# A hybrid decoder layer on one core: gate strips ahead of branch strips, the recurrence's last step behind the convolution, and evenly spaced head steps

## The reference

```
xn = rmsnorm(x)
p  = xn @ w_in                      # 2048 x 13328, split into xl, gl, q, k, v, z, b, a, u_pool, three gates
xl = causal_conv(xl, width 4)       # then the RG-LRU recurrence h_t = a_t h_{t-1} + b_t
o_lru  = h * gelu(gl)
o_dn   = gated delta rule over 8 heads of 128, on conv'd q, k, v, then a norm and silu(z)
o_pool = causal means over 2, 4, 8, 16 tokens, a grouped product, a scale
merged = sum over the three branches of sigmoid(gate_b) * (o_b @ w_back_b)
x = x + merged @ w_out
x = x + square(relu(rmsnorm(x) @ w_up)) @ w_down
y = rmsnorm(x)                      # and the states of all branches
```

## Time and profile before

| what | us |
|---|---|
| median of 3 runs | 2188.42 (2185.13 to 2188.83) |
| the profiled execution | 2186.87 |
| its span in the trace | 2185.1 |
| PE busy (products) | 2149.7, 98% of the span |
| DVE / ACT / POOL busy | 1222.3 / 784.2 / 175.9 |
| granted clock of PE, mean over the span | 0.994 |
| first gated pass (RG-LRU branch) | from about 324 |
| second gated pass (pooling branch) | from about 654 |

### The profile page before, as it was taken

The page is one execution under the profiler, slowest core; times in us unless marked ns, Lnnn a source line. Parts: engine busy times, 40 slices in busy tenths (PEclk is TensorE's granted clock), DMA queues, the critical chain, the costliest instruction groups (busy, mean ns, idle before and its releaser), DMA issues.

```text
span 2185.1 us, 35787 instructions
## 1 busy us (share of the span) xinstructions
PE 2149.7 (98%) x14515; PEld 2094.4 (96%) x14515; DVE 1222.3 (56%) x1996; ACT 784.2 (36%) x946; POOL 175.9 (8%) x340
## 2 busy tenths in 40 slices
PE   9999998999999999999999999999999999999997
PEld 9998997999998999999999999999999999999997
DVE  7996785555566655555454554444444444444444
ACT  6434553222232222333334343333333333333343
POOL 7000012110022110010000000000000000000001
PEclk9999999999999999999999999999999999999998
DMA  6544443343353433336544444444444444444443
GB/s 218 163 143 128 140 129 121 116 119 116 116 165 106 118 117 116 116 107 212 150 148 155 145 144 152 147 153 146 154 145 154 146 154 146 154 145 154 147 144 106
DMA packets 295609, 308.96 MB, mean 141 GB/s; under 512 B 9712, under 2 KB 290416, under 8 KB 295232
## 3 DMA queue, kind: packets, MB, share of 16 engines
q1 hardware_dynamic: 291616, 291.54, 43.1%
q0 software_dynamic: 3584, 15.55, 2.4%
q10 hardware_dynamic: 288, 0.15, 0.0%
HBM read 298.83 MB, written 8.37 MB: 141 GB/s over the span
## 4 chain that ended last, share of the span: by engine, by line
PE 84%; DVE 9%; ACT 3%; issue 3%; DMA 1%; DVEq 0%; ACTq 0%; SPq 0%
PE main L1436 26%; PE main L1438 25%; PE main L1437 25%; PE aux L1556 6%; DVE scratch L892 2%; DVE lo L885 2%; DVE scratch L885 2%; ACT hi L617 1%; DMA raw<-in_w_in 1%; DVE scratch L889 1%; PE aux L1539 0%; PE aux L1529 0%; DVE scratch L888 0%; DVE merged L885 0%; PE aux L1660 0%
## 5 line engine op out<-in xcount | busy, mean ns | idle before, releaser
L885 DVE TENSOR_TENSOR lo<-raw,hi 128x1024 fp32r<-128x1024 f32 x546 | 667.2, 1230 | 566.6 <-ACT hi L617 560.0
L617 ACT ACTIVATE hi<-raw 128x1024 fp32r<-128x1024 f32 x546 | 573.3, 1056 | 920.6 <-PE main L1438 904.8
L1436 PE MATMUL main<-x_hi,hi 128*128 128x320 f32 x2688 | 842.8, 314 | 2.5 <-DVE x_lo L892 2.0
L1438 PE MATMUL main<-x_hi,lo 128*128 128x320 f32 x2688 | 831.5, 309 | 0.0
L1437 PE MATMUL main<-x_lo,hi 128*128 128x320 f32 x2688 | 831.5, 309 | 0.0
L1436 PEld LDWEIGHTS main<-x_hi,hi 128*128 128x128 f32 x2688 | 505.7, 188 | 10.6 <-issue 5.0
L1437 PEld LDWEIGHTS main<-x_lo,hi 128*128 128x128 f32 x2688 | 505.8, 188 | 0.7
L1438 PEld LDWEIGHTS main<-x_hi,lo 128*128 128x128 f32 x2688 | 505.4, 188 | 0.0
L1436 PE MATMUL main<-o_hi,hi 128*128 128x320 f32 x1408 | 444.6, 316 | 4.6 <-DVE o_lo L885 4.6
L1438 PE MATMUL main<-o_hi,lo 128*128 128x320 f32 x1408 | 435.6, 309 | 0.0
L1437 PE MATMUL main<-o_lo,hi 128*128 128x320 f32 x1408 | 435.5, 309 | 0.0
(11 more groups left out here) (253 smaller groups left out, 1190.8 us busy)
## 6 DMA issues: line engine op xcount, KB each, us to landing
raw<-in_w_in SPq DMA_DIRECT2D x210, 512.0 KB, 3.8
raw<-in_w_up SPq DMA_DIRECT2D x128, 512.0 KB, 3.8
raw<-in_w_down SPq DMA_DIRECT2D x128, 512.0 KB, 3.4
raw<-in_w_back SPq DMA_DIRECT2D x80, 512.0 KB, 3.4
scratch<-in_s_in POOLq DMA_DIRECT2D x8, 512.0 KB, 4.7
out_s_out<-scratch POOLq DMA_DIRECT2D x8, 512.0 KB, 4.6
merged<-in_x SPq DMA_DIRECT2D x8, 320.0 KB, 7.8
qkv<-in_x POOLq DMA_DIRECT2D x1, 2560.0 KB, 10.2
```

Source lines behind the costliest of these rows:

```text
L617: act.activation(HI[:, slot * TILE:(slot + 1) * TILE], RAW[:, slot * TILE:(slot + 1) * TILE], ACT.Copy).then_inc(hi_ready, 1)
L885: return dve.tensor_tensor(out, a, b, op)
L1436: pe.matmul(bank, hi, xh, start=first, stop=False)
L1438: return pe.matmul(bank, lo, xh, start=False, stop=last)
```

## The change

It does four things.

1. In a gated turn both gate strips run first (tiles 0 to 3 and 4 to 7, banks 0, 1 and 2, 3), then both branch strips (tiles 8, 9 and 10, 11). There is a gate buffer for each strip; the rows RN and BG now lie in the first. Gate 0 and gate 1 are at keys 8 and 12, merge 0 and merge 1 at keys 2 and 4 of the next turn. SP's loads follow that order.
2. In the recurrence part step 5 moves from key 7 to key 8, on DVE behind `lru_conv`, on ACT behind the split that stands at key 7 already (`walk_ahead` has none left at key 8). Turn 3's steps, which run in the first gated turn, keep key 7.
3. The 19 steps of head i of a pass are placed by a formula in tiles of the whole pass, 5.5 + 10.9 i for k0, + 0.8 for k1, + 2.1 for k2, then 0.48 a step from + 2.6. Heads no longer coincide with turns.
4. The loops over turns 1 to 3 of the first two gated passes are written out on PE, ACT and DVE.

```diff
-        GS = sb("gate", 2 * N)
-        RN, BG = sb("qk_scale_rows", N), sb("beta_gamma_rows", N)
+        GS, GS1 = sb("gate", 2 * N), sb("gate_second", 2 * N)
+        GATE = (GS, GS1)
+        RN, BG = GS[:, 0:N], GS[:, N:2 * N]
...
             def gated(it, n0, name):
                 for s in range(2):
                     for j in range(4):
-                        load(n0, 12, it, 6 * s + j, A["w_in"], j * 512, it * 512 + (G0[name] + s * 256))
+                        load(n0, 12, it, 4 * s + j, A["w_in"], j * 512, it * 512 + (G0[name] + s * 256))
+                for s in range(2):
                     for j in range(2):
-                        load(n0, 12, it, 6 * s + 4 + j, A["w_back"], BACK[name] + j * 512, it * 512 + s * 256)
+                        load(n0, 12, it, 8 + 2 * s + j, A["w_back"], BACK[name] + j * 512, it * 512 + s * 256)
...
-        def lru_steps(step, it):
+        def lru_steps(step, it, last=7):
 
             return {pos: [lambda k=k: step(it, k) for k in ks]
-                    for pos, ks in ((3, (0,)), (4, (1,)), (5, (2, 3)), (6, (4,)), (7, (5,)))}
+                    for pos, ks in ((3, (0,)), (4, (1,)), (5, (2, 3)), (6, (4,)), (last, (5,)))}
...
-        def dn_place(k, peeled):
-
-
-            if peeled and k < 14:
-                return ((5, 3), (6, 1), (6, 4), (6, 6), (7, 0), (7, 2), (7, 4), (7, 6), (7, 7),
-                        (8, 1), (8, 2), (8, 4), (8, 6), (8, 7))[k]
-            if k < 6:
-                return ((1, 7), (2, 5), (3, 7), (4, 2), (4, 5), (4, 7))[k]
-            return (5 + (k - 6) // 2, (3, 7)[k % 2]) if k < 18 else (11, 6)
-
-        def dn_steps(step, h, peeled, late):
+        def dn_place(i, k):
+
+            at = 5.5 + 10.9 * i + ((0.0, 0.8, 2.1)[k] if k < 3 else 2.6 + 0.48 * (k - 3))
+            eighth = int(round(8 * at))
+            return (eighth - 1) // 8, (eighth - 1) % 8
+
+        def dn_steps(step, h0, it):
 
             steps = {}
-            for k in range(19):
-                pos = dn_place(k, peeled)[0] + 4
-                if (pos > 12) == late:
-                    steps.setdefault(pos - 12 * late, []).append(lambda k=k: step(h, k))
+            for i in range(4):
+                for k in range(19):
+                    at = dn_place(i, k)[0] + 4 - 12 * it
+                    if 0 < at <= 12:
+                        steps.setdefault(at, []).append(lambda i=i, k=k: step(h0 + i, k))
             return steps
...
-                lru(it, lru_steps(lru_step, it - 1))
+                lru(it, lru_steps(lru_step, it - 1, 8))
...
-                walk(split, LRU_N, 8, it, 8, {**after, 8: [lambda: lru_conv(it)]})
+                walk(split, LRU_N, 8, it, 8, joined({8: [lambda: lru_conv(it)]}, after))
...
-            def gated(it, n0, t0, g0, h0, branch, after, peeled=False):
-                own = {8: [lambda: gate(n0, t0, it, 0)], 10: [lambda: merge(n0, t0, g0, it, 0, branch)]}
+            def gated(it, n0, t0, g0, h0, branch, after):
+                own = {8: [lambda: gate(n0, t0, it, 0)], 12: [lambda: gate(n0, t0, it, 1)]}
                 if h0 is not None:
-                    own = joined(own, dn_steps(dn_step, it + h0, peeled, False))
+                    own = joined(own, dn_steps(dn_step, h0, it))
                 walk(split, n0, 12, it, 12, joined(after, own))
 
             def late(it, n0, t0, g0, h0, branch):
 
-                steps = {2: [lambda: gate(n0, t0, it, 1)], 4: [lambda: merge(n0, t0, g0, it, 1, branch)]}
-                return steps if h0 is None else joined(steps, dn_steps(dn_step, it + h0, False, True))
+                steps = {2: [lambda: merge(n0, t0, g0, it, 0, branch)], 4: [lambda: merge(n0, t0, g0, it, 1, branch)]}
+                return joined(steps, dn_steps(dn_step, h0, 4)) if h0 is not None and it == 3 else steps
...
                 for s in range(2):
-                    strip(n0, 12, t0, 8, it, 6 * s, 4 * s, XH, XL, between=between)
-
-                    strip(n0, 12, t0, 8, it, 6 * s + 4, 4 * s + 2, OH, OL,
+                    strip(n0, 12, t0, 8, it, 4 * s, 2 * s, XH, XL, between=between)
+                for s in range(2):
+                    strip(n0, 12, t0, 8, it, 2 * s + 8, 2 * s + 4, OH, OL,
                           waits=(lambda i: (o_ready, o0 + 2 * (i + 1))) if first is not None and s == 0 else None,
                           tiles=2, between=between)
 
-            gated(0, GPL_N, GPL_T, 0, 4, 0)
-            with pe.Fori(1, 4) as it:
+            gated(0, GPL_N, GPL_T, 0, 4, 0, dn_first=4)
+            for it in range(1, 4):
                 gated(it, GPL_N, GPL_T, 0, None, 0)
```

More of the change, by code:

```diff
@@ L767, in dn_step, with gated @@
                     act.activation(S1, AX[2][:, 0:P], ACT.Copy).then_inc(s1_ready, 1)
-            def gated(it, n0, t0, h0, after, peeled=False):
-                own = {8: [lambda: gate(it, 0, t0, 0)]}
-                if h0 is not None:
-                    own = joined(own, dn_steps(dn_step, it + h0, peeled, False))
-                walk(split, n0, 12, it, 12, joined(after, own))
-            def late(it, t0, h0):
-                steps = {2: [lambda: gate(it, 1, t0, 0)]}
-                return steps if h0 is None else joined(steps, dn_steps(dn_step, it + h0, False, True))
-            gated(0, GPL_N, GPL_T, 0, lru_steps(lru_step, 3), True)
-            with act.Fori(1, 4) as it:
-                gated(it, GPL_N, GPL_T, 0, late(it - 1, GPL_T, 0))
+            def gated(it, n0, t0, h0, after):
+                own = {8: [lambda: gate(it, 0, t0, 0)], 12: [lambda: gate(it, 1, t0, 0)]}
+                walk(split, n0, 12, it, 12, joined(after, joined(own, dn_steps(dn_step, h0, it))))
+            gated(0, GPL_N, GPL_T, 0, lru_steps(lru_step, 3))
+            for it in range(1, 4):
+                gated(it, GPL_N, GPL_T, 0, {})
             def pool_hi(g):
@@ L786, in pool_hi @@
                 act.activation(OH[:, 2 * g * N:2 * (g + 1) * N], DD, ACT.Copy).then_inc(ohi_ready, 1)
[L788 to L791, removed]
+            walk(split, POOL_N, 16, 0, 16, {**dn_steps(dn_step, 0, 4), 12: [lambda: pool_hi(0)], 16: [lambda: pool_hi(1)]})
+            gated(0, GPP_N, GPP_T, 4, {4: [lambda: pool_hi(2)], 8: [lambda: pool_hi(3)]})
+            for it in range(1, 4):
+                gated(it, GPP_N, GPP_T, 4, {})
             def o_squares():
@@ L1306, in _ @@
             walk(split, POOL_N, 16, 0, 16, steps)
-            gated(0, GPP_N, GPP_T, 8, 4, 1, {4: [lambda: pool_out(2), lambda: pool_sums(3)], 8: [lambda: pool_out(3)]},
-                  True)
-            with dve.Fori(1, 4) as it:
-                ch.enter(it, 1, LINKS["gpp"])
+            gated(0, GPP_N, GPP_T, 8, 4, 1, {4: [lambda: pool_out(2), lambda: pool_sums(3)], 8: [lambda: pool_out(3)]})
+            for it in range(1, 4):
                 gated(it, GPP_N, GPP_T, 8, 4, 1, late(it - 1, GPP_N, GPP_T, 8, 4, 1))
-                ch.leave(3, "gpp")
             def o_norm():
@@ L1631, in dn_step, with gated @@
                     ins.then_inc(fin_psum, 1)
[L1633 removed]
+            def gated(it, n0, t0, h0, first, o0, between=None, dn_first=None):
                 between = dict(between or {})
                 if h0 is not None:
[L1636 to L1638 removed]
+                    for i in range(4):
+                        for k in range(19):
+                            j, b = dn_place(i, k)
+                            if it * 12 <= j < it * 12 + 12:
+                                between[j - 12 * it] = list(between.get(j - 12 * it, ())) + [
+                                    (b, lambda i=i, k=k: dn_step(h0 + i, k, dn_first if i == 0 else None))]
                 for s in range(2):
[L1640 to L1642 removed]
+                    strip(n0, 12, t0, 8, it, 4 * s, 2 * s, XH, XL, between=between)
+                for s in range(2):
+                    strip(n0, 12, t0, 8, it, 2 * s + 8, 2 * s + 4, OH, OL,
                           waits=(lambda i: (o_ready, o0 + 2 * (i + 1))) if first is not None and s == 0 else None,
                           tiles=2, between=between)
[L1646 to L1647 removed]
+            gated(0, GPL_N, GPL_T, 0, 4, 0, dn_first=4)
+            for it in range(1, 4):
                 gated(it, GPL_N, GPL_T, 0, None, 0)
@@ L1667, in _ @@
                                15: [(7, lambda: pool_product(2))]})
-            gated(0, GPP_N, GPP_T, 4, 8, 4, {3: [(7, lambda: pool_product(3))]})
-            with pe.Fori(1, 4) as it:
+            gated(0, GPP_N, GPP_T, 4, 8, 4, {3: [(7, lambda: pool_product(3))]}, dn_first=8)
+            for it in range(1, 4):
                 gated(it, GPP_N, GPP_T, 4, None, 4)
```

45 lines of the change are left out of this document (19 added, 26 removed).

## The result

The changed kernel takes 2203.88 us (median of 4 runs, 2201.59 to 2208.56); the kernel before took 2187.81 beside it (4 runs, 2185.13 to 2188.83). The ratio is 1.0083, 95% interval 1.0071 to 1.0095: **slower by 16 us**. The profiled execution took 2203.09 (span 2201.3), 16.2 more in the span than the one before. The forecast was 2215 with a range of 2196 to 2231 and 0.84 on slower.

The account below looks back on a forecast made before the run. PE, busy 98% of the span, bounds the kernel. Losses after of 59.9 (recurrence 11.1, first pass 25.8, second 23.0) less 31 before add 28.6 to 29 to 2186.87: 2215 us, range 2196 to 2231.

Parts of the forecast that it names:

- The recurrence: Step 5 behind the convolution: 4.4 of PE waits go, 11.1 of waits on lo and low clock come, plus 6.7.
- Rival (c): Only the head places fail; the recurrence gains 4.4 instead of losing 6.7: 2204, chance 0.12.
- k0 behind the late o_ready: First gated pass, first head: k0 waits 6.9 for head_rows plus 1.6 low clock, 8.5 where 6.6 was before.
- The places: Head steps drift to eighths where DVE's results come late: 36.6 of stalls and 3.2 of clock over two passes.
- k3 and k15 of head 3: Longest head stalls: k3 3.5 behind late key copies, k15 1.7 behind lo and merge, 2.65 in the second pass.
- k3 of heads 1 and 2: First pass: PE waits for copies after lt_ready, one lo fewer and no gate behind it, stalls 1.1 and 1.4.
- the stalls of the heads: PE waits within the heads of the gated passes: 15.7 in the first pass, 20.9 in the second.
- the 31 of before: Kernel before: PE waits in the touched stretches plus low clock, about 31 us, the most the change can win.
- The order of the gates: Gates first: the 4.6 wait at o_lo goes, but k0 still waits for o_ready: 8.5 for 6.6.
- (a): The drift of head steps is harmless, DVE reaches each before it is needed: 2176, faster, chance 0.09.
- (b): Every PE idle of 0.7 or more throttles the clock, some 19 more stretches of 1.6: 2245, chance 0.05.
- (d): The parts cancel: half of the small stalls, no low stretches, 2188 to 2191, no change, chance 0.05.

Follow-up runs that it names:

- the fastest kernel: Changed kernel with step 5 at key 1 of the next turn, ACT's key copies one step later, head steps at 76 listed places: 2158.13 us, ratio 0.9868.

## Why the prediction was right

**The recurrence.** Forecast: 4.4 of waits gone, three waits of a main product on lo of 3.1, 3.1 and 1.7 to 1.8 in their place, and a low stretch behind the first two; 6.7 more in all. Measured: 2.82, 2.80 and 1.31, each 0.16 longer than shown, so 2.98, 2.96 and 1.47. The first product began at 262.45 where the chain had 262.3. Only one low stretch came: in the window from 296.9, behind the second wait, the clock is 1.00. So it is 7.4 and 1.7, 9.1 instead of 11.1, 4.7 more than before; as a part of its own it measured 5.6 and 6.3. How many come is not settled by these waits: of five kernels with the same two waits of 2.80 to 2.82, two have a low stretch behind the first alone, one behind the second alone and two behind both. Rival (c), that the recurrence gains, falls. Its 2204 is the measured time by chance: it is lower than the forecast by 11 in the recurrence, and the measured time is so mainly in the heads.

**k0 behind the late o_ready.** Forecast 6.9 and 1.6 of clock. Measured 6.28, 6.4 with the tail, and a low stretch of 10.2, of which PE idled until 355.04 and worked 6.46, half of it lost: 3.2. That is 9.7 instead of 8.5. The clock was the mis-sized term.

**The places.** Forecast 36.6 of stalls and 3.2 of clock over the two passes. The waits on L877, L1193 and L1613 are 20.9 in 25, 24.9 with their 0.16 each; some twenty that I had at 0.1 to 0.4 don't appear, and a modelled end can cover up to 0.16 of each, 3 at most. One low stretch (556), 1.7. The order of the list is right: k3 and k15 of head 3 wait longest, each 0.16 longer than shown: 1.72 and 1.39 in the first pass for 3.5 and 1.7 forecast, 1.73 and 2.38 in the second for 3.5 and 2.65. The waits of heads 0 to 2 lie at their steps, k3 of heads 1 and 2 at 0.79 and 0.92 (forecast 1.1 and 1.4).

**The term that was mis-sized** is the stalls of the heads, 36.6 for a measured 25 to 28. The largest single error in it is k3 of head 3, 1.9 for 3.5 in each pass, and there the reason failed too. I put 8.7 from dn_done to the masked decay, as in the earlier trace rows. In the changed kernel it is 539.44 to 546.06, 6.6: the second store had landed after 3.03 of waiting on POOL, where the kernel before has 5.09:

```profile
410.20 0.90 POOL L458 DMA_DIRECT2D scratch<-in_s_in  x1 [5.09 <-DMA out_p_out<-scratch]
```

POOL was done before DVE needed it: DVE works from 546.47, when PE's k1 had ended, to 549.42 without a stop. So lt was ready 1.2 before PE's k2 began (550.66), where I had k2 wait for it, and the chain from lt to the copies took 5.5 and not 5.9: the stall is 1.9 and not 3.5. The parts of that chain (copies 0.87, two hi, two lo, gate, copies) stand in the trace as they were written down. The rest of the error, some 5 to 9 us over both passes, is in small stalls that were shorter than forecast or don't appear, and no run takes them apart.

**The sum.** After: recurrence 9.1, k0 9.7 and 0.5 in the second pass, heads 24.9 to 28, clock 1.7: 46 to 49, less the 31 of before is 15 to 18; the spans differ by 16.2. The forecast's 59.9 was 11 to 14 too high: 9 to 12 in the heads, 1.5 in their clock, 2.0 in the recurrence, and 1.2 the other way at k0. So the direction and the places of the waits were right, and the size of the loss, 28.6, was nearly twice the measured one. From the parts: the order of gates alone minus 2.2, the step behind the convolution plus 6.2 on it (2190.73 less 2184.58), the places plus 13.2. These make 17.2, with 16.1 to 17.1 between the changed kernel and the medians of before.

**The order of the gates** was forecast as a loss of about 2 (8.5 for 6.6) and gains 2.2. The wait before k0 was right within 0.7. One thing was missing, the merge that leaves the chain of k1 to k3 of the first head: of the 5.0 at k2 the order took 1.5, and the new places the other 3.5, which the kernel with the old places still has. The forecast put all of it down to the places. What else the 2.2 are made of stays open, as said above.

**The other rivals.** (a), the drift is harmless, falls: 25 waits in the heads, and 13.2 us come back with the old places. (b), every idle of 0.7 or more throttles, falls: the window from 880 to 930 holds waits of 1.73, 0.84 and 2.38 at a clock of 1.00. The Trainium skill, "TensorE: Matmul & The Clock Gate", section on HAM oscillation, describes waits that recur with each group of products and throttle each time; in its example each wait is longer than the group's work, and the short idles that the prediction had in mind are in the section behind it. No stretch of this trace shows it, with 16 waits in one group of steps and three low stretches in all. (d), the parts cancel, falls: one does gain, but by 2.2 against 19.4.

## What to carry to other kernels

Before moving a step to relieve one engine, follow the other engine that waits for its result: what matters is what stands behind that wait in its own order, here the hi of the next tile behind o_hi (7.4 us of waits) and behind the key copies (6.0 us). Moving the waiting instruction one position further, behind the hi of the next tiles, was worth 9.2 and 7.2 us with the clock, with the work on PE as it was (in the 9.2 are the table loads that went with the loops, and with the listed places it was 6.3). Spreading steps evenly is not spacing them by what each needs: the formula's 10.9 tiles a head cost 13 us against hand-set places, and a list made from the engines' timetable, with the later key copies, wins 23 over these; how much of it is the copies' is not known.

## What was not expected of the hardware

- Idles of the same length had different clocks behind them: 2.82 us at 262.45 brought a stretch of 3.4 at the lower level, 2.80 at 297.25 and 2.38 at 922.08 none, and 1.72 at 554.98 one of 3.4. In the kernel with the listed places and the step behind the convolution both waits of 2.80 brought one, and with the key copies later only the second did. What decides it stays open, and a forecast for one kernel can miss by 1.7 us for each.
- The length of a stretch at the lower level does not follow the idle before it: 3.4 us behind 4.59 in the kernel before and behind 2.82 in the changed one, 10.2 with 6.28 (begun within the idle, 3.8 of it idle), 6.8 behind 2.65 in the fastest kernel.
- The landing of the same two stores of a head, as POOL sees it, differs with where the steps of the heads stand: POOL waited 5.0 to 5.3 us for it in all six cases of the kernel before, 5.0 to 6.4 with the old places and the gates first, 3.0 to 3.9 in all six of the changed kernel, and 3.2 to 5.8 with the listed places. What makes it shorter was not tried. It is enough to take the sum from dn_done to the masked decay from 8.7 to 6.6.
